# Attention input projections as seven-product blocks in a stage of their own, the last output projection in the same form, and the result in four transfers

## What is computed

```python
q, k, v, g = split(h @ w_in)            # 1024 -> 2048, 1024, 1024, 2048
q = rope2d(rmsnorm(q, q_g)); k = rope2d(rmsnorm(k, k_g))
kc, vc = split(hc @ w_in[:, 2048:4096]) # context keys and values
kc = rmsnorm(kc, k_g)                   # no rotation
o = softmax(q @ [kc; k].T / sqrt(128)) @ [vc; v]   # 16 query heads, 8 key heads
x = x + gate * ((o * silu(g)) @ w_out)
y = layernorm(depthwise_conv(a * sigmoid(b)))       # second convolution
x = x + gate * ((silu(y) * silu(c)) @ conv_w_out)
return rmsnorm(x, final_g)
```

## Time and profile before

| what | value |
|---|---|
| timed runs | 4115.13 us median, 4114.27 to 4117.16 |
| profiled execution, its own time | 4119.65 us |
| its span, first to last instruction | 4117.8 us |
| mean granted TensorE clock | 0.985 |
| PE busy | 3873.4 us, 94% |
| DVE, ACT, POOL busy | 2212.9, 955.8, 992.8 us |
| chain that ended last | PE 27%, nearly all of it matmuls into `lin_ps` |
| HBM read, written | 277.52 MB, 30.41 MB |

### The profile page before, as it was taken

The page is one execution under the profiler, slowest core; times in us unless marked ns, Lnnn a source line. Parts: engine busy times, 40 slices in busy tenths (PEclk is TensorE's granted clock), DMA queues, the critical chain, the costliest instruction groups (busy, mean ns, idle before and its releaser), DMA issues. The chain is left out here.

```text
span 4117.8 us, 75565 instructions
## 1 busy us (share of the span) xinstructions
PE 3873.4 (94%) x33254; PEld 2703.5 (66%) x33254; DVE 2212.9 (54%) x3428; ACT 955.8 (23%) x1755; POOL 992.8 (24%) x749
## 2 busy tenths in 40 slices
PE   6999999999999999999998888888899999999997
PEld 3488888758888855555555777787655555557443
DVE  2577725668785149836443455555424444453693
ACT  1411100110110020021014444444213444441102
POOL 0144544104444420001332223322010001014200
PEclk9999999999999999999999999999999999999998
DMA  2133323423442212112324211110201111111221
GB/s 72 57 113 140 106 83 129 167 112 123 143 143 82 72 51 61 41 41 77 108 93 165 96 35 35 39 49 17 82 31 59 57 44 54 57 39 52 72 72 41
DMA packets 152192, 320.05 MB, mean 78 GB/s; under 512 B 15936, under 2 KB 111168, under 8 KB 141120
## 3 DMA queue, kind: packets, MB, share of 16 engines
q1 hardware_dynamic: 148144, 304.81, 21.8%
q0 software_dynamic: 3728, 10.49, 1.0%
HBM read 277.52 MB, written 30.41 MB: 75 GB/s over the span
## 5 line engine op out<-in xcount | busy, mean ns | idle before, releaser
L931 PE MATMUL lin_ps<-hn,ring 128*128 128x256 f32 (+1 forms) x3968 | 1272.5, 476 | 20.5 <-ACT arena L1876 9.1
L931 PEld LDWEIGHTS lin_ps<-hn,ring 128*128 128x128 f32 x3968 | 750.3, 190 | 493.1 <-issue 431.9
L931 PE MATMUL lin_ps<-arena 64*64 64x64 f32 (+5 forms) x9784 | 701.6, 258 | 78.0 <-ACT arena L1876 32.7
L931 PE MATMUL lin_ps<-arena,ring 128*128 128x256 f32 (+1 forms) x2784 | 705.0, 409 | 11.2 <-DVE arena L2928 7.6
L931 PEld LDWEIGHTS lin_ps<-arena 64*64 64x64 f32 (+2 forms) x9784 | 532.2, 144 | 177.0 <-issue 94.7
L931 PEld LDWEIGHTS lin_ps<-arena,ring 128*128 128x128 f32 x2784 | 531.6, 192 | 154.5 <-issue 82.5
L1876 ACT ACTIVATE arena<-lin_ps 128x512 f32<-128x512 f32 (+3 forms) x491 | 248.2, 527 | 913.3 <-PE lin_ps L931 881.9
L2472 DVE SCALAR_TENSOR_TENSOR arena<-arena,vec 128x512 f32<-128x512 f32 (+3 forms) x499 | 392.6, 861 | 1.3
L2472 DVE SCALAR_TENSOR_TENSOR arena<-arena,cs 128x512 f32<-128x512 f32 x336 | 345.3, 1095 | 0.0
L931 PE MATMUL sum_ps<-arena 64*64 64x64 f32 (+1 forms) x7176 | 309.7, 224 | 21.9 <-issue 14.1
L931 PEld LDWEIGHTS sum_ps<-arena 64*64 64x64 f32 (+1 forms) x7176 | 261.2, 137 | 36.3 <-issue 22.4
(11 more groups left out here) (253 smaller groups left out, 4564.8 us busy)
## 6 DMA issues: line engine op xcount, KB each, us to landing
ring<-w_up SPq DMA_DIRECT2D x32, 1024.0 KB, 5.8
ring<-w_down SPq DMA_DIRECT2D x32, 1024.0 KB, 5.0
arena<-w_mod SPq DMA_DIRECT2D x24, 1024.0 KB, 7.7
arena<-w_mod SPq DMA_DIRECT2D x12, 2048.0 KB, 7.8
features<-arena SPq DMA_DIRECT2D x64, 384.0 KB, 6.2
ring<-w_attn SPq DMA_DIRECT2D x16, 1536.0 KB, 6.6
ring<-w_conv_in SPq DMA_DIRECT2D x16, 1024.0 KB, 5.7
ring<-features SPq DMA_DIRECT2D x40, 384.0 KB, 3.4
```

Source lines behind the costliest of these rows:

```text
L931: return pe.matmul(out, lhsT, rhs, start=start, stop=stop)
```

## The change

The 8 rounds become two stages. In the first (`attn_p`), 24 pairs in the blocked form run in the order of `ATTN_ORDER`: eight of keys with values, eight of query heads, eight of gates. The context's keys and values stay plain (`context`). Keys and values of all heads stay in SBUF; queries and gates are made in turning buffers, stored by SP to a scratch tensor in HBM (16 stores of 512 KB) and read back one head at a time in the second stage (32 loads of 256 KB). The second stage has the 64 units alone, with two score buffers, three buffers of weights, `turn` two units behind `scores`, and `weigh` spread over four units. Task banks move from `lin_ps` to `sum_ps` and `out_ps` (four in place of two). The first weights of `attn_out` are loaded once the second head's loads are issued. `conv1_out` takes the blocked form with 4 pairs, its first pair in the order with an early S1 product. The result leaves in four transfers of two blocks each. The rotation of a pair is moved by POOL's queue after the weight sums of the third chunk behind it. The diff, cut to its core (weight layouts, semaphores and buffer addresses are left out):

```diff
+ATTN_ORDER = ["kv0", "q0", "kv1", "q1"]
+for _r in range(2, 8):
+    ATTN_ORDER += [f"kv{_r}", f"q{_r}", f"g{_r - 2}"]
+ATTN_ORDER += ["g6", "g7"]
...
+            def keep_made(n):
+
+                name, r = ATTN_ORDER[n], int(ATTN_ORDER[n][-1])
+                f, sem_ = (0, q_stored) if name[0] == "q" else (1, g_stored)
+                if name[0] == "q":
+                    sp.wait_ge(qk_ready, 3 * r + 3)
+                else:
+                    sp.wait_ge(gated_g, USED + r + 1)
+                if r:
+                    sp.wait_ge(sem_, USED + 16 * r)
+                to = scratch[2 * f + 2 * r // KD, 2 * r % KD:2 * r % KD + 2, :, 0:SEQ].rearrange("a p n -> p a n")
+                sp.dma_start(to, made(name)).then_inc(sem_, 16)
...
+                        if name == "attn_p":
+                            for n_ in (step - 4, step - 5):
+                                if n_ >= 0 and ATTN_ORDER[n_][0] == ("q" if n_ == step - 5 else "g"):
+                                    keep_made(n_)
...
+                if name == "attn":
+                    first, last = Q["attn_p"].chunk1, len(ATTN_ORDER)
+                    for step in range(last, last + 5):
+                        for n_ in (step - 4, step - 5):
+                            if n_ < last and ATTN_ORDER[n_][0] == ("q" if n_ == step - 5 else "g"):
+                                keep_made(n_)
+                    for h in range(HEADS):
+                        sp.wait_ge(q_stored, USED + 16 * (h // 2 + 1))
+                        if h >= 2:
+                            sp.wait_ge(sc_mm, QB * (h - 1))
+                        sp.dma_start(head_q[h % 2], kept(0, h)).then_inc(q_in[h % 2], 16)
+                        sp.wait_ge(g_stored, USED + 16 * (h // 2 + 1))
+                        if h >= 2:
+                            sp.wait_ge(hd_ev, h - 1)
+                        sp.dma_start(head_g[h % 2], kept(1, h)).then_inc(g_in[h % 2], 16)
+                        if h == 1:
+                            for n in range(first, first + 3):
+                                sp.wait_ge(chunk_mm, n - 2)
+                                step = n - first
+                                w = t["w_attn_out"][step // 2, :, 2048 * (step % 2):2048 * (step % 2) + 2048]
+                                sp.dma_start(raw_slot(n), w).then_inc(raw_full[raw_turn(n)], 16)
...
-            sp.wait_ge(h_ready, 80)
-            sp.dma_start(t["out"].rearrange("(k p) n -> p k n", p=P), xs[:, :, CTX:ALL]).then_inc(out_sem, 16)
-            sp.wait_ge(out_sem, 16)
+            for k in range(0, KD, 2):
+                sp.wait_ge(h_ready, 8 * NI["last"] + k + 2)
+                sp.dma_start(t["out"].rearrange("(k p) n -> p k n", p=P)[:, k:k + 2, :], xs[:, k:k + 2, CTX:ALL]).then_inc(out_sem, 16)
+            sp.wait_ge(out_sem, 64)
...
+                if i:
+                    pe.wait_ge(lin_ev, S["conv1_g"].tile1)
+                    for p in range(Q["conv1_out"].pairs):
+                        pair_products("conv1_out", p, 0, conv_out_b, out_need)
+                    return
...
+            def context(n):
+
+                r, c = int(ATTN_ORDER[n][2]), Q["attn_p"].chunk0 + n
+                pe.wait_ge(raw_full[raw_turn(c)], raw_count(c))
+                to = take_bank(r, "ctx")
+                w = raw_slot(c).rearrange("p (k n) -> p k n", k=KD)
+                for v in range(2):
+                    for k in range(KD):
+                        if n == 0 and v == 0:
+                            pe.wait_ge(h_ready, 8 * NI["at"] + k + 1)
+                        m = mm(to[:, CTX * v:CTX * v + CTX], w[:, k, P * v:P * v + P], hn[:, k, 0:CTX], k == 0, k == KD - 1)
+                m.then_inc(pj_mm, 1)
...
+            def beside_pair(n):
+
+                key, r = ATTN_ORDER[n][0], int(ATTN_ORDER[n][-1])
+                if key == "k":
+                    square_sum(r, "sks", 1, aksq[:, CTX:ALL])
+                    square_sum(r, "skc", 1, aksq[:, 0:CTX])
+                    pe.wait_ge(pj_ev, task_no(r, "ctx") + 1)
+                    pe.wait_ge(bank_ev, bank_free(Q["attn_p"].pair0 + n + 1))
+                    turn_v(r, "va", range(2, KB))
+                    turn_v(r, "vb", range(2))
+                if key == "q":
+                    square_sum(r, "sq0", 2, asq[:, 0, :])
+                    square_sum(r, "sq1", 3, asq[:, 1, :])
...
+            for n in range(len(ATTN_ORDER)):
+                if ATTN_ORDER[n][0] == "k":
+                    context(n)
+                pair_products("attn_p", n, 0, attn_p_b, attn_p_need)
+                if n:
+                    beside_pair(n - 1)
...
+                pe.wait_ge(sc_ev, max(U - 1, 0))
                 for c0, cw in SEGS[ALL]:
-                    m = mm(lin_ps[:, score_buf(U), 256 + c0:256 + c0 + cw], aq[r % 2][:, a, q * P:(q + 1) * P], ak[r % 2][:, c0:c0 + cw], True, True)
+                    m = mm(score_ps[U % 2][:, c0:c0 + cw], head_q[h % 2][:, q * P:(q + 1) * P], ak[h // 2][:, c0:c0 + cw], True, True)
...
+            pe.wait_ge(bank_ev, bank_free(Q["attn_p"].pair1))
+            pe.wait_ge(pj_ev, len(ATTN_TASKS))
+            for U in range(UNITS + 6):
+                if U < UNITS:
                     scores(U)
-                    fill(r + 1, i, 0)
-                    if U:
-                        turn(U - 1)
-                    fill(r + 1, i, 1)
-                    if i == 3 and r:
-                        weigh(2 * r - 1)
-                    if i == 7:
-                        weigh(2 * r)
-            turn(UNITS - 1)
-            weigh(HEADS - 1)
+                if 2 <= U < UNITS + 2:
+                    turn(U - 2)
+                if U >= 6:
+                    weigh((U - 6) // QB, [(0, 1), (2, 3), (4,), (5,)][(U - 6) % QB])
...
+            def made_pair(n):
+
+                key, r = ATTN_ORDER[n][0], int(ATTN_ORDER[n][-1])
+                act.wait_ge(bank_ev, bank_free(Q["attn_p"].pair0 + n + 1))
+                if key == "k":
+                    act.wait_ge(pj_ev, task_no(r, "ctx") + 1)
+                    f(aksq, ak[r], ACT.Square).then_inc(pj_sq, 1)
+                if key == "q":
+                    for h in range(2):
+                        f(asq[:, h, :], made(ATTN_ORDER[n])[:, h, :], ACT.Square).then_inc(pj_sq, 1)
+                if key == "g":
+                    f(made_g, made_g, ACT.Silu).then_inc(gated_g, 1)
...
+            for n in range(len(ATTN_ORDER)):
+                if ATTN_ORDER[n][0] == "k":
+                    take_context(int(ATTN_ORDER[n][2]))
+                take_p1(Q["attn_p"].pair0 + n)
+                if n:
+                    made_pair(n - 1)
+                    beside_pair(n - 1)
...
+            for U in range(UNITS + 2):
+                if U >= 2:
+                    take_turned(U - 2)
+                if U < UNITS:
+                    exps(U)
...
+                    if i and k == 5:
+                        dve.wait_ge(conv_out, 8 * i + 4)
+                        block_sums(conv_out_b[0], (1,))
...
+                    if key == "q" and r >= 2:
+                        dve.wait_ge(q_stored, USED + 16 * (r - 1))
+                    if key == "g" and r:
+                        dve.wait_ge(g_stored, USED + 16 * r)
+                b = Q["attn_p"]
+                take_pair(b.pair0 + n, b.chunk(n, 0) + 1, (top[:, lo_t], top[:, hi_t]), (low[:, lo_t], low[:, hi_t]))
...
+            for n in range(len(ATTN_ORDER)):
+                if n >= 2:
+                    normalize(n - 2)
+                attn_pair(n)
+                if n >= 2:
+                    rotated(n - 2)
...
+            for U in range(UNITS + 1):
+                if U < UNITS:
                     dve.wait_ge(sc_mm, U + 1)
                     o.wait()
-                    o(nc.vector.tensor_reduce(small[:, 0:1], scs, AXX, ALU.max))
+                    o(nc.vector.tensor_reduce(small[:, 0:1], score_ps[U % 2], AXX, ALU.max))
                     o.wait()
                     o(nc.vector.tensor_scalar(small[:, 2 + U % 2:3 + U % 2], small[:, 0:1], -ATT_SCALE, None, ALU.mult), neg)
-                    if i == 0:
-                        rotated(r, 2)
-                        if r:
-                            head_out(2 * r - 2)
-                    if i == 4 and r:
-                        head_out(2 * r - 1)
-                    if i in (1, 2, 4, 6) and r == s.rounds - 1:
-                        if i == 1:
-                            dve.wait_ge(hd_ev, 8)
-                        block_sums(attn_out_b[0], ([1, 2, 4, 6].index(i) + 1,))
-                    beside_unit(r + 1, i)
-                    dve.wait_ge(sc_ev, U + 1)
+                if U:
+                    dve.wait_ge(sc_ev, U)
                     o.wait()
-                    o(nc.vector.reciprocal(small[:, 6:7], small[:, 4 + U % 2:5 + U % 2]))
+                    o(nc.vector.reciprocal(small[:, 6:7], small[:, 4 + (U - 1) % 2:5 + (U - 1) % 2]))
                     o.wait()
```

(45 more changed lines are left out.)

373 lines of the change are left out of this document (159 added, 214 removed).

## The result

The changed kernel took 4066.41 us (median of 4 runs, 4064.9 to 4071.75), beside 4116.15 us for the kernel before on the same chip (4 runs, 4114.27 to 4126.69). The ratio is 0.9871, 95% [0.9859, 0.9884]. Forecast were 4063.5 us, between 4049 and 4083.

The account below looks back on a forecast made before the run. PE, busy 94% of the span, was taken as the bound. Attention 44.4 us earlier, second convolution's projection 3.3 and result 4.0 sum to 51.7 us, from the profiled 4119.65 and less a 4.5 offset to 4063.5; range 4049 to 4083.

Parts of the forecast that it names:

- Stage one: Block-form attention products: 46.8 us of PE work a round instead of 51.8, eight rounds 374.6 us; called the gain's core, 39.8 us.
- ACT's table loads: Near the attention's start, table loads of 1.28 us delay two context banks: 2.6 us, between 0 and 5.
- (b): Rival in stage one: DVE late because POOL works in every pair, PE waits for a bank, 4071 to 4087; chance 0.05.
- The seam: Between the last pair and the first scores, PE stands 7 us (5 to 14) for last gates and first queries.
- The clock's price: Behind the stop between the last pair and the first scores, a low clock costs 3 us (0 to 6).
- Stage two: The 64 units keep their old 206.6 us of PE work; PE stays the limit at 3.23 us a unit on average.
- the head loads: Stage two: queries queued behind gates on SP land 0.6 us late for each of 14 heads, 8 us (0 to 30).
- The second convolution's projection: `conv1_out` in block form: 48.4 us of products for 55.0, less 1.9 at the start and 1.4 at the end; net 3.3.
- The result: At the kernel's end, four output transfers instead of one let the first leave earlier: 4 us saved (2 to 4.5).
- (a): Rival in stage two: head loads land in 4.4 us, each head stops 2.1 us, 30 instead of 8, so 4085; chance 0.08.
- (c): Rival: stage two bound by the round from scores over DVE and ACT to transposes, 4.85 us a unit, 4154; chance 0.04.
- (d): Rival: the clock falls again and again in stage two, once a head at 3 us, 48 us, so 4111; chance 0.03.

Follow-up runs that it names:

- the control: The changed kernel itself, with no edit, run again on the chip of the first group of experiments: 4055.59 us, ratio 0.9863 to the kernel before.

## Why the prediction was right

**Stage one** came out as worked out: 375.0 us for 374.6 of matmuls, and an eighth product cost 41.15 for 41.3. The 2.6 us for ACT's table loads did not occur; that term was sized wrong, at the lower end of its 0 to 5. DVE was busy 151.5 of 200 us, that is 35 of a round's 46.8, against 29.3 in the prediction. The rotation was costed by a row of before, whose POOL makes no weight sums beside the projections; with them the rotation's first multiplication has a median of 1522 ns for 692. It cost nothing, as DVE still had 11 us a round to spare, and rival (b) falls for this kernel. Its mechanism, PE waiting for DVE to empty a bank, shows only with 175 us of POOL in 200, and then for 3.6 us in all.

**The seam**: 5.6 us for the 7 forecast, and the wait was the one named: loading the queries before g7 is stored took it away. The clock's price of 3 us is confirmed twice, by 6.91 for 3.87 us of scores, and by 3.1 us less when idle products kept PE busy.

**Stage two**: from the first scores 223.95 us. The prediction's own terms for it are 206.6, 3 for the clock, 4 for the first units, 1 and 8 for the head loads, 222.6. Of these the head loads were argued from 0.6 us for each head, through SP's order and a landing time of 3.0. The pace shows 0.72 a head (13.64 less 12.92) at a landing of 3.1, and in the control 0.54 at 2.8; undoing it gave 8.45. Mechanism and size were right. What would have misled is the wait's label: a reader of the list of waits would have looked for it in PE. The first units waited 1.14 us at `turn`, and 3.2 us in all, for 4.

**The second convolution's projection**: 3.3 us predicted, from 6.6 of products less 1.9 at the start and 1.4 at the end. At equal clock the runs show 6.55, 1.8 and 1.3, net 3.45, so the working was right term by term. The 4.5 between the two traces and the 2.8 of the run with the plain form differ from it by how long the clock stayed low in each execution. The argument "the longer stop meets a clock that is already low, so no further price" held: the low clock cost 1.8 us in the kernel after and 2.0 to 2.9 in the other eight traces with this stretch unchanged, for 2.8 and 1.4 in the two with the plain form. That filling the stop brings 2.0 us shows a price that both kernels pay.

**The result**: 4.0 for 4.

**From the profiled time to the median.** This step has no footing. The prediction took off 4.5 us, because the profiled execution of before stood so far above its median. After, the profiled execution (4066.18) and the median (4066.41) agree. By its own sum the prediction gave 4068.0 for a profiled execution, 1.8 us too high, and 4063.5 for the median, 2.9 too low. The timed runs of the kernel before alone spread from 4114.27 to 4126.69, so the offset is no larger than the scatter of one execution. The close hit on the total is partly luck. By the stretches the change is worth 55.2 us, 3.5 more than the 51.7 of the sum; the medians of this pair differ by 49.7, those of the control's group by 57.1.

**The rivals.** (a) falls: a head stopped 0.5 to 0.7 us, not 2.1. (b) falls, above. (c) does not occur with the lag of two units, but is real with one, and dearer than its price: 5.4 us a unit by work and waits (3.23 and 2.16) and 6.7 in all (429.56 / 64), where the prediction had 4.85. (d) does not occur: the granted clock is 1.00 over 180 us of stage two, transposes and all. The Trainium skill (TensorE: Matmul & The Clock Gate, "Part 4: PE-mode transpose") says that transposes don't count for the clock as other matmuls do; with PE busy 174 of 180 us, a fifth of it in transposes, no cost of that shows here. With one unit of lag the clock did fall again and again, so (d)'s mechanism exists, and it came with PE's idle time: the transposes are the same as in the control. The two rivals were thus not apart, as the prediction had them: a chain that leaves PE idle for a third of the time also loses the clock, 77 us of it beside 130 of standing still.

## What to carry to other kernels

Where PE is full, count its columns and the stops; the block form paid what its arithmetic says. Compare two forms at the same clock: behind a stop of PE, how long the clock stays low differed by 1.4 us between two executions of the same matmuls. Where work is taken out from between dependent steps, keep a lag deep enough that PE never waits: each 2.16 us of waiting cost 3.2 in all. When a queue waits for two kinds of buffers, put first what PE needs first: two such reorderings on SP gave 15.6 us of the attention for no work at all. A stop in PE labelled "issue" that returns at a fixed point of a loop may be a wait: here it was a load in stage two, and DVE's emptying of a bank in the run with more work on POOL.

## What the runs showed of the hardware

With `turn` one unit behind, PE was busy 39.06 of 60 us, in spans of 3 to 4 us with stops of 2.16 us between them, and the granted clock went between 1.00 and 0.50 again and again. It stayed at 1.00 in a window with PE busy 7.10 of 10 and in the first units of the run with the early queries, 4.74 of 6. Behind one and the same stop of 3.42 us the same 64 matmuls took 57.93 us in one execution and 56.56 in another. DVE multiplications of 128x512 with both inputs in SBUF took up to 4327 ns beside POOL and 695 at most before, while reciprocals (3344 and 3340 ns) and adds with one input in PSUM (424 and 424) did not change with 73 us more of POOL in 200. The start of the attention, behind the same instructions, moved by 13 us between executions; why, was not studied.
